# One instruction for bias and minimum, and scores issued four heads at a time, in a neighbourhood attention

## What is computed

```python
s_nb = jnp.einsum('bchd,bicjhd->bhcij', q_r, k_win) + bias   # keys in the window of the query
s_cx = jnp.einsum('bchd,blhd->bhcl', q_r, k_c)               # context keys
p = jax.nn.softmax(jnp.concatenate([s_nb, s_cx], axis=-1).astype(jnp.float32), axis=-1)
o = p_nb @ v_win + p_cx @ v_c
```

## Time and profile before

| what | value |
|---|---|
| median of three runs | 2332.44 us (2331.81 to 2334.12) |
| the profiled execution's own time | 2329.71 us |
| its span in the trace | 2327.6 us |
| PE, DVE, ACT, POOL busy | 84%, 40%, 30%, 4% |
| mean granted clock of TensorE | 0.938 |
| attention, from the first transposes to the projection | 852.9 to 905.7 us |
| from about 1400 us to the end | expert weights, 427 GB/s |

### The profile page before, as it was taken

One profiled execution on the slowest core, in us unless ns is written; L12 is line 12 of the kernel. 1 busy time (PEld: TensorE's weight loads), 2 busy tenths in 40 slices (PEclk: granted clock), 3 DMA queues, 4 the chain that ended last, 5 costly groups with the idle time before them and its releaser, 6 DMA issues.

```text
span 2327.6 us, 38292 instructions
## 1 busy us (share of the span) xinstructions
PE 1946.0 (84%) x16711; PEld 1467.0 (63%) x16711; DVE 930.4 (40%) x1634; ACT 687.7 (30%) x1253; POOL 93.8 (4%) x112
## 2 busy tenths in 40 slices
PE   6998899999999999999998999666666576666666
PEld 4996667888788887999896476433333343333433
DVE  4446745433524246665666365333111121111111
ACT  4334435222424246554553322111111011111111
POOL 0011110000001011000200000000000000000000
PEclk9999999999999999999999999888888888888889
DMA  6316553221225224444530359999999999999997
GB/s 277 145 37 274 199 226 131 78 109 53 97 96 217 109 74 173 177 165 150 217 121 10 157 207 397 426 427 427 427 427 427 427 426 427 427 427 427 428 427 311
DMA packets 48007, 592.29 MB, mean 254 GB/s; under 512 B 5934, under 2 KB 6890, under 8 KB 12001
## 3 DMA queue, kind: packets, MB, share of 16 engines
q1 hardware_dynamic: 44416, 580.21, 60.8%
q0 software_dynamic: 2992, 8.57, 1.2%
q10 hardware_dynamic: 432, 1.06, 0.1%
HBM read 588.77 MB, written 1.05 MB: 253 GB/s over the span
## 4 chain that ended last, share of the span: by engine, by line
PE 47%; DMA 29%; DVE 6%; ACT 4%; issue 2%; POOL 0%; SPq 0%; DVEq 0%; ACTq 0%; POOLq 0%
DMA s_ring<-in_w_up 14%; PE bank L725 10%; PE bank L727 10%; PE bank L726 10%; DMA s_arena<-in_w_up 6%; PE bank L1458 5%; DMA s_xT<-in_w_up 4%; DMA s_hT<-in_w_up 3%; DVE s_ring_r L2416 2%; ACT s_arena_r L1694 2%; PE bank L1494 2%; DMA s_xT<-in_w_down 1%; PE bank L1445 1%; PE bank L1277 1%; PE bank L1500 1%
## 5 line engine op out<-in xcount | busy, mean ns | idle before, releaser
L725 PE MATMUL bank<-s_arena_r 128*128 128x256 f32 (+2 forms) x1858 | 603.9, 325 | 8.5 <-DVE s_hT_r L2421 3.9
L727 PE MATMUL bank<-s_arena_r,s_ring_r 128*128 128x256 f32 (+2 forms) x1514 | 499.7, 330 | 0.0
L1694 ACT ACTIVATE s_arena<-bank 32x256 f32<-32x256 f32 (+6 forms) x418 | 167.9, 407 | 1001.7 <-PE bank L1458 536.9
L1458 PE MATMUL bank<-s_ring,s_arena 128*32 128x256 f32 x1952 | 281.0, 506 | 143.2 <-DMA s_hT<-in_w_up 40.3
L726 PE MATMUL bank<-s_hT_r,s_arena_r 128*128 128x512 f32 (+2 forms) x1200 | 399.3, 333 | 0.0
L725 PEld LDWEIGHTS bank<-s_arena_r 128*128 128x128 f32 x1858 | 347.9, 187 | 46.0 <-issue 8.9
L2416 DVE TENSOR_TENSOR s_ring_r<-s_ring,s_arena_r 128x2048 fp32r<-128x2048 f32 (+3 forms) x120 | 247.8, 2077 | 273.7 <-ACT s_arena_r L1694 273.6
L727 PEld LDWEIGHTS bank<-s_arena_r,s_ring_r 128*128 128x128 f32 x1514 | 284.8, 188 | 28.8
L1458 PEld LDWEIGHTS bank<-s_ring,s_arena 128*32 128x32 f32 x1952 | 136.0, 144 | 218.4 <-issue 205.8
L1694 ACT ACTIVATE s_arena_r<-s_ring 128x2048 fp32r<-128x2048 f32 (+3 forms) x120 | 206.2, 1730 | 153.5 <-PE bank L727 123.6
L726 PEld LDWEIGHTS bank<-s_hT_r,s_arena_r 128*128 128x128 f32 x1200 | 225.3, 188 | 24.1 <-issue 0.5
(11 more groups left out here) (398 smaller groups left out, 2505.2 us busy)
## 6 DMA issues: line engine op xcount, KB each, us to landing
s_ring<-in_slabs SPq DMA_DIRECT2D x68, 2048.0 KB, 8.3
s_ring<-in_w_down SPq DMA_DIRECT2D x32, 2048.0 KB, 28.9
s_ring<-in_w_up SPq DMA_DIRECT2D x31, 2048.0 KB, 33.7
s_ring<-in_w_gate SPq DMA_DIRECT2D x30, 2048.0 KB, 33.2
s_arena<-in_w_gate SPq DMA_DIRECT2D x16, 2048.0 KB, 33.5
s_arena<-in_w_up SPq DMA_DIRECT2D x16, 2048.0 KB, 33.2
s_arena<-in_w_down SPq DMA_DIRECT2D x14, 2048.0 KB, 28.8
s_ring<-in_slabs SPq DMA_DIRECT2D x16, 1408.0 KB, 6.1
```

What stands on the lines that cost most here:

```text
L725: mm(out, w_hi_, x_hi_, start=start, stop=False, skip_group_check=skip)
L727: return mm(out, w_lo_, x_hi_, start=False, stop=stop, skip_group_check=skip)
L1458: last = mm(pb[b][32 * q:32 * q + 32, 0:256], x[:, c, :], (gate, up)[q // 2](c, q % 2), start=c == 0, stop=c == DC - 1, skip_group_check=True)
L1694: return act.activation(out, in_, func, **kw)
```

## The change

VectorE's two instructions of `na_add` become one: it writes `(scores + bias) * -1` and gives the minimum of that, started from 3.0e38, as its accumulator output. `na_max` is gone; ScalarE waits for `na_add`, which is now raised when the minimum is there too. And TensorE issues no scores behind `na_out` of an even step; behind an odd step j it issues those of pairs j + 2 and j + 3. Pairs 4, 6, ... 14 so keep their place, and pairs 3, 5, ... 15 come one step later than before.

```diff
                 if j >= 1:
                     na_out(j - 1)
-                if j + 3 < NA_H:
-                    na_scores(j + 3)
+                if j % 2:
+                    for k in range(j + 2, min(j + 4, NA_H)):
+                        na_scores(k)
...
             def na_exp(i):
-                act.wait_ge(S["na_max"], i + 1)
+                act.wait_ge(S["na_add"], i + 1)
...
-                STT(out=n_s[i % 6], in0=NA_BANK[i % 4][:, :], scalar=-1.0, in1=n_bias[:, i % 4, :], op0=ALU.mult, op1=ALU.subtract).then_inc(S["na_add"], 1)
-                dve.wait_ge(S["na_add"], i + 1)
-                dve.tensor_reduce(n_mx[:, i % 6, 0:1], n_s[i % 6], AX_X, ALU.min).then_inc(S["na_max"], 1)
+                dve.tensor_tensor_reduce(out=n_s[i % 6], in0=NA_BANK[i % 4][:, :], in1=n_bias[:, i % 4, :], scale=-1.0, scalar=3.0e38,
+                                         op0=ALU.add, op1=ALU.min, accum_out=n_mx[:, i % 6, 0:1]).then_inc(S["na_add"], 1)
```

## The result

The changed kernel took 2336.45 us in the median of 22 runs (2332.5 to 2339.96), against 2331.65 us for the kernel before in 22 runs beside it: a ratio of 1.0016, 95% interval 1.001 to 1.0022, that is 2.3 to 5.1 us slower (3.7 by the ratio itself, 4.8 by the two medians). One of the 22 runs of the kernel before was a slow one of 3730.81 us and is left out of the ratio; the others took 2329.16 to 2336.98. The forecast was +3.0 us and 2335.4.

What follows compares the result with a forecast made beforehand. The prediction took TensorE to bound the attention, with VectorE slack. Its terms 1.95 + 0.2 + 0.85 gave +3.0 us, moving the median from 2332.44 to 2335.4 us, with a range of 2331.0 to 2340.5.

Steps and rivals of the forecast that it cites:

- fused instruction alone: VectorE's `na_add` in the attention: faster work only widens VectorE's idle time, gain by itself 0.
- a unit on VectorE, start to start: Fused `na_add`: one unit was to take 0.68 us of VectorE in place of 1.33.
- `na_out` free to start by VectorE, behind the scores: Double step: VectorE's adds, reciprocal and `na_shared` were to release `na_out` 2.93 us after the scores start.
- second pair of a double issue saves: TensorE's scores: the second pair skips the entry into the shape and costs 0.88 us, saving 0.18.
- stall in a step without scores: TensorE waits 0.57 us before the second transposes for ScalarE's copy, which stands behind `na_read`.
- five twos of steps: Steps 2 to 11: each two steps take 7.03 us, not 6.64, 0.39 more; five make +1.95 us.
- steps 0 and 1: Start of the attention: pair 3's scores move and the doubled scores come in, +0.2 us.
- the end, pair 15 late: Pair 15 comes behind step 13, so `na_out(13)` waits for `na_shared(11)` behind its adds: +0.85 us.
- attention: Sum over the attention part of the kernel: +3.0 us, its end moving from 905.7 to 908.7.
- rival built on a slow instruction: Double steps: fused instruction slower than 0.70 us makes `na_out` wait for VectorE; 0.85 gives +4.8 us; chance 0.21.
- The path through VectorE: Double step, scores start to `na_out`: adds start at 1.16, two units 1.36, reciprocal 0.08, `na_shared` and semaphore 0.33.
- TensorE's own 2.96: Double step: TensorE reaches `na_out` 2.96 us after the scores start, by 1.06 + 0.88 + 1.02.

Runs made afterwards that it cites:

- e1: Changed kernel with scores issued one pair a step as before, so only the fused instruction remains; attention 53.85 us, median 2330.95 us, ratio 0.9994 to the kernel before.
- e4: Changed kernel with ScalarE's `na_read` moved behind the copy of unit 2j+1; attention 51.67 us, median 2332.14 us, ratio 0.9999 to the kernel before.
- e7: Changed kernel with pair 15's scores issued behind step 12, not step 13; attention 55.89 us, median 2336.96 us, ratio 1.0015 to the kernel before.
- e8: Changed kernel with three small reciprocals added behind every fused instruction to slow VectorE; attention 58.51 us, median 2339.87 us, ratio 1.0028 to the kernel before.
- e3: Changed kernel unaltered, measured again on the chip of the others; attention 56.68 us, median 2334.38 us, ratio 1.0008 to the kernel before.
- e5: Changed kernel with scores one pair a step as before and `na_read` behind the copy of unit 2j+1; attention 51.83 us, median 2331.18 us, ratio 0.9997.
- e9: Changed kernel with doubled scores behind even steps, late `na_read` and VectorE's two instructions back; attention 50.89 us, median 2329.96 us, ratio 0.9989 to the kernel before.
- e2: Kernel before with only the doubled scores behind odd steps, VectorE keeping two instructions; attention 66.45 us, median 2345.2 us, ratio 1.0055 to the kernel before.
- e10: Changed kernel with doubled scores behind even steps, fused instruction and `na_read` at its old place; attention 56.01 us, median 2336.73 us, ratio 1.0015.
- e6: Changed kernel with doubled scores behind even steps and `na_read` behind the copy of unit 2j+1; attention 50.62 us, median 2328.79 us, ratio 0.9984.

## Why the prediction was right, step by step

The time fell into the range, the sign was that of the forecast, and the mechanism is the one named. The parts, in the order of the sum:

| step | predicted | measured | read from |
|---|---|---|---|
| fused instruction alone | 0 | 0.00 | e1 |
| a unit on VectorE, start to start | 0.68 | 0.61 | changed kernel |
| `na_out` free to start by VectorE, behind the scores | 2.93 | 903.66 - 900.84 = 2.82 | changed kernel, pair 15 |
| second pair of a double issue saves | 0.18 | 2 x 1.06 - 1.92 = 0.20 | changed kernel |
| stall in a step without scores | 0.57 | 7.01 - (6.65 - 0.20) = 0.56 | changed kernel; e4 removes it |
| five twos of steps | +1.95 | +1.81 | chain, 860.69 to 895.75 |
| steps 0 and 1 | +0.2 | +0.23 | chain, 853.99 to 860.69 |
| the end, pair 15 late | +0.85 | +0.79 | chain from 895.75; e7 |
| attention | +3.0 | +2.83 | |

**The mis-sized price was the accumulator.** It is handed out by an instruction of its own, as the rule of the Trainium skill has it ("VectorE: DVE Perf Modes", section "Two Vector instructions with no wait between them"), 0.08 us long; but the next instruction starts at the same moment (874.51 twice in the fence above), so it costs VectorE nothing from start to start. I had added 0.07 for each unit. The rival built on a slow instruction was therefore never near: 0.61 against its point of 0.85. The Trainium skill's rule for two 32-bit sources in SBUF ("Vector Engine (DVE) Microarchitecture Reference", section "Points that are easy to get wrong") could not decide it, as one source was a PSUM bank. Nor is the halving seen where both sources are in SBUF and no accumulator is asked for: SCALAR_TENSOR_TENSOR over 128x256 in float32 takes 0.42 us in the median with both in SBUF (L2606 of the kernel before, 16 times) and 0.48 with one in PSUM (L2643, 48 times). e8 shows that the rival's mechanism was right, only not its condition.

**Two sums came out better than their terms.** The path through VectorE was put at 1.16 + 1.36 + 0.08 + 0.33. It was 1.09 + 1.23 + 0.08 + 0.42. The 1.16 took the start of the scores from the timeline (873.85), while TensorE's own 2.96 went by the chain of waits, where they start at 873.91; and the 0.06 for the last semaphore was 0.14. So the slack in a double step was not 0.03 us but 2.94 - 2.82 = 0.12. And behind pair 15 the wait is 2.82 - 2.08 = 0.74, not 0.85; that the end still came to +0.79 is in part luck, as products that start afresh take 0.07 more (1.09 and not 1.02), a term the sum lacks.

**What the attention does not explain.** The median difference was 4.8 us, 3.7 by the ratio, the attention's 2.83. That the median of 2336.45 lies only 1.05 from the forecast is helped by a kernel before that was 0.8 us faster here than the 2332.44 that the forecast started from. With e3 the repeated comparison gave a median difference of 1.4. Over all ten experiments the time follows the attention within the intervals, on either side of it. So I take the remaining 1 to 2 us of the first comparison for the spread outside the attention, of which the last section shows one cause; no run ties them to the change.

**What I left out was the way out.** The prediction read in the earlier trace rows that the kernel before already stalls in its last steps, priced the stall at 0.57, and then only counted how often the change repeats it. The same rows said that nearly 2 us lay there; one moved instruction brought 2.0 (e5, with the fused instruction in place), more than either half of the change could.

## What to carry to other kernels

A fused instruction on an engine that waits for another one buys no time; here it bought slack, and whether an order is good depends on whether that slack is enough, so work out the latest place first (`na_out` against `na_shared`) and not the busy shares. When work is batched on the engine that sets the pace, look at what it covered in the step that it leaves: 1.06 us of scores hid a wait of 0.57 for ScalarE, and their removal cost nearly three times what the batch saved (0.20). Steps at the end of a loop, where a part of the work has run out, show such uncovered paths in the trace of before.

## What the hardware showed that was not expected

**The same code ahead of the attention differs by 2 us and more from run to run, along with the granted clock.** The attention starts at 851.9 us in the profile before and at 854.0 in the changed kernel's, though nothing ahead of it but its first four units differs. In the windows of 200 to 220 us the granted clock is 1.00 in one and 0.91 in the other: pieces of it were granted half speed, 1.2 GHz, in the second. But little of the 2.1 us arises there. One line of VectorE (L2643 before, L2644 changed) runs many times; the same execution of it starts at 200.09 and 200.69 us in the two profiles, a later one at 218.96 and 219.81, the next at 221.76 and 224.12. So 0.6 us were there before, and most of the rest, 1.5 us, comes right behind the window, where the granted clock of 220 to 224 us is 1.00 before and 0.57 in the changed kernel. In all twelve profiles the two go together: in the three with 1.00 in both stretches the attention starts at 851.0 to 852.2 us, and at 853.1 to 856.8 in the nine others, which have 0.83 to 0.91 in 200 to 220 us and 0.50 to 0.78 in 220 to 224. No run sets the clock, so which follows from which is not shown. It is not the new instruction: e5, which has it, ran at 1.00 there, and e9, which has not, at 0.91. In order before, changed, e5, e9:

```profile
200.00:220.00 20.00, 14.95 (x212) 10.81 (x213) 17.15 (x31) 9.61 (x28) 5.45 (x4) 1.00 0.80 322
```
```profile
200.00:220.00 20.00, 15.94 (x208) 11.31 (x208) 16.88 (x30) 9.38 (x28) 5.44 (x4) 0.91 0.83 335
```
```profile
200.00:220.00 20.00, 14.92 (x212) 10.78 (x213) 17.00 (x30) 9.42 (x27) 5.45 (x4) 1.00 0.81 322
```
```profile
200.00:220.00 20.00, 15.87 (x210) 11.29 (x208) 17.18 (x30) 9.70 (x28) 5.43 (x4) 0.91 0.84 342
```

The 4 us behind it, before and changed:

```profile
220.00:224.00 4.00, 4.00 (x98) 3.26 (x100) 3.26 (x8) 1.27 (x2) 0.00 (x0) 1.00 0.02 6
```
```profile
220.00:224.00 4.00, 3.79 (x12) 2.51 (x12) 1.95 (x6) 2.08 (x4) 0.00 (x0) 0.57 0.00 0
```

TensorE is busy 15 to 16 of the 20 us, in pieces with waits between; in the attention, even with its stalls, the clock stayed at 1.00. Taking the attention off each profiled time leaves 2273.4 us (e2) to 2282.7 us (e10) for the rest of the program, in kernels that share that rest: 9 us of spread, three times the effect studied. A profile's own stretch told 0.8 us apart (e7) where the times of nine runs could not.

**A block of scores costs 0.20 us beyond its products, half on each side.** Two single issues take 2.12 us, a double one 1.92, with the same instructions. The changed kernel's trace shows where the difference lies: the products of a double issue start at 872.73, 873.26, 873.69 and 874.12 (two heads at a time, 0.01 apart), and the transposes behind them at 874.65. The steps are 0.53, 0.43, 0.43 and 0.53; in a single issue both are 0.53. So 0.10 is lost where the scores begin and 0.10 where the next array shape begins. `na_out` has a like price: its 16 products take 1.02 us behind the transposes, and 0.87 in e6 where they follow L1105, which has their shape (903.44). No run tells the change of shape from the first load of weights, which comes with it here.
